# Spreading the forget-gate sums of eight attention heads to all partitions: products and copies, or DMAs from one row

## What is computed

```python
def forgetting_attention(q, k, v, f_logit):
    """logit[t,s] = q_t.k_s / sqrt(Dh) + sum_{s<j<=t} log sigmoid(f_logit_j), for s <= t."""
    logf = jax.nn.log_sigmoid(f_logit.astype(jnp.float32))
    c = jnp.cumsum(logf, axis=1).transpose(0, 2, 1)
    ...
        logits = jnp.einsum('bqhd,bkhd->bhqk', qb, kb).astype(jnp.float32) * scale
        logits = logits + c[:, :, q0:q1, None] - c[:, :, None, :q1]
        logits = jnp.where(causal[None, None], logits, -jnp.inf)
        p = jax.nn.softmax(logits, axis=-1).astype(v.dtype)
        outs.append(jnp.einsum('bhqk,bkhd->bqhd', p, vb))
```

## Time and profile before

| | us |
|---|---|
| median of 3 timed runs | 2202.22 |
| lowest and highest | 2200.33, 2208.86 |
| the profiled execution | 2198.62 |
| its span on the core | 2196.8 |
| TensorE busy in it | 2107.9 (96%) |
| VectorE busy | 1241.9 (57%) |
| ScalarE busy | 832.4 (38%) |
| POOL busy | 204.6 (9%) |

### The profile page before, as it was taken

The page is one execution under the profiler, slowest core; times in us unless marked ns, Lnnn a source line. Parts: engine busy times, 40 slices in busy tenths (PEclk is TensorE's granted clock), DMA queues, the critical chain, the costliest instruction groups (busy, mean ns, idle before and its releaser), DMA issues.

```text
span 2196.8 us, 26815 instructions
## 1 busy us (share of the span) xinstructions
PE 2107.9 (96%) x10738; PEld 1653.3 (75%) x10738; DVE 1241.9 (57%) x1891; ACT 832.4 (38%) x1335; POOL 204.6 (9%) x173
## 2 busy tenths in 40 slices
PE   6999999999999999998999999999999989999998
PEld 5777887678878876665788888777777767888886
DVE  4555665436677777887544344465675754443443
ACT  4344554345323233125423223344554543232231
POOL 2222001011000004452000000100000000000001
PEclk9999999999999999999999999999999999999999
DMA  5212322124677762652242332122121221422321
GB/s 175 77 58 96 117 96 77 39 77 154 240 251 251 269 244 89 151 148 74 77 135 93 99 96 96 52 78 58 43 74 49 62 92 58 134 96 96 96 96 39
DMA packets 217530, 241.74 MB, mean 110 GB/s; under 512 B 9920, under 2 KB 203968, under 8 KB 211264
## 3 DMA queue, kind: packets, MB, share of 16 engines
q1 hardware_dynamic: 207616, 229.58, 32.0%
q10 hardware_dynamic: 9792, 10.45, 1.9%
HBM read 229.01 MB, written 2.10 MB: 105 GB/s over the span
## 4 chain that ended last, share of the span: by engine, by line
PE 82%; DVE 8%; ACT 6%; issue 2%; ACTq 1%; DMA 1%; POOL 1%; DVEq 0%; SPq 0%; POOLq 0%
PE bank L1170 22%; PE bank L1171 22%; PE bank L1172 22%; PE bank L1191 2%; PE bank L1193 2%; PE bank L1192 2%; DVE wL L1751 1%; PE bank L1368 1%; PE bank L1345 1%; PE bank L1241 1%; DVE hX L2093 1%; PE bank L1254 1%; PE bank L1234 1%; PE bank L1296 1%; ACTq L1595 1%
## 5 line engine op out<-in xcount | busy, mean ns | idle before, releaser
L1170 PE MATMUL bank<-hH,wH 128*128 128x512 f32 (+1 forms) x1672 | 663.8, 397 | 33.1 <-DVE hL L1757 16.2
L1171 PE MATMUL bank<-hL,wH 128*128 128x512 f32 (+1 forms) x1672 | 647.7, 387 | 0.0
L1172 PE MATMUL bank<-hH,wL 128*128 128x512 f32 (+1 forms) x1672 | 647.7, 387 | 0.0
L1404 ACT ACTIVATE wH<-raw 128x1024 fp32r<-128x1024 f32 (+1 forms) x378 | 335.0, 938 | 363.4 <-PE bank L1172 267.6
L1751 DVE TENSOR_TENSOR wL<-raw,wH 128x1024 fp32r<-128x1024 f32 (+1 forms) x342 | 377.7, 1147 | 165.7 <-ACT wH L1404 165.6
L1170 PEld LDWEIGHTS bank<-hH,wH 128*128 128x128 f32 x1672 | 316.2, 189 | 124.4 <-issue 51.3
L1172 PEld LDWEIGHTS bank<-hH,wL 128*128 128x128 f32 x1672 | 315.9, 189 | 64.9
L1171 PEld LDWEIGHTS bank<-hL,wH 128*128 128x128 f32 x1672 | 316.4, 189 | 62.9 <-issue 2.4
L1170 PE MATMUL bank<-hidH,wH 128*128 128x512 f32 x768 | 299.2, 390 | 3.4 <-DVE hidL L1911 3.4
L1172 PE MATMUL bank<-hidH,wL 128*128 128x512 f32 x768 | 298.8, 389 | 0.0
L1171 PE MATMUL bank<-hidL,wH 128*128 128x512 f32 x768 | 298.8, 389 | 0.0
(11 more groups left out here) (214 smaller groups left out, 2059.3 us busy)
## 6 DMA issues: line engine op xcount, KB each, us to landing
raw<-in_mlp SPq DMA_DIRECT2D x64, 1024.0 KB, 5.3
araw<-in_ada_w SPq DMA_DIRECT2D x48, 1024.0 KB, 5.0
raw<-in_w_ff SPq DMA_DIRECT2D x32, 1024.0 KB, 7.3
raw<-in_hgrn_in SPq DMA_DIRECT2D x32, 512.0 KB, 3.8
raw<-in_w_in SPq DMA_DIRECT2D x12, 1024.0 KB, 5.3
raw<-in_conv_in SPq DMA_DIRECT2D x16, 512.0 KB, 4.8
u<-uc ACTq DMA_DIRECT2D x120, 67.5 KB, 3.1
raw<-in_w_mv SPq DMA_DIRECT2D x4, 1024.0 KB, 5.7
```

The costliest lines, as they stand in the source:

```text
L1170: mm(out, wH[:, s, m:m + 128], xh[:, k, 0:width], start=k == 0, stop=False)
L1171: mm(out, wH[:, s, m:m + 128], xl[:, k, 0:width], start=False, stop=False)
L1172: i = mm(out, wL[:, s, m:m + 128], xh[:, k, 0:width], start=False, stop=k == KB - 1)
L1404: do(wH[:, s, c], raw[:, r, c], ACT.Copy).then_inc(*s_whi.up(n, x))
```

## The change

The eight products and the eight copies go, with `sel` and its load. Item `decay` is now a DMA on SP's queue: it reads the row of head h from `tmp` (a source of one partition, repeated 128 times by a step of 0) and writes it to 128 partitions. There are four places for a head: the two slots of `cneg` and the last two key blocks of `qk` (12 + sc, that is 14 and 15), which are not filled until the key columns of the last heads are computed; `ev_k` for those two blocks now waits for POOL's last bias of heads 6 and 7. The DMAs of pair p + 1 are appended when pair p starts, those of pair 0 just before. The third and fourth pair's wait until POOL is done with the head that had the place. The first two `rel` loads move one pair forward. The minus sign, which `sel` gave, is moved into `ev_gate`: same instructions with other operations.

The diff, without the parts that only rename:

```diff
+    def decays(self, p):
+
+        for h in (2 * p, 2 * p + 1):
+            self.chead[0, h] = 2 * (p % 2) + h % 2
+            self.do("decay", h=h, sc=self.chead[0, h], n=p // 2 + 1,
+                    cfree=(("pool", "bias", (0, h - 4, 3)),) if p > 1 else ())
+
+    def rels(self, p):
+        for h in (2 * p, 2 * p + 1):
+            self.chead[1, h] = h % 2
+            self.do("rel", h=h, sc=h % 2, after=(("dve", "max", (1, h - 2, 3)) if p else ("pool", "bias", (0, h + 4, 3)),))
+
     def pairs(self):
+        self.decays(0)
         for g in range(2):
             for p in range(4):
-                for h in (2 * p, 2 * p + 1):
-                    sc, free = self.cslots.get()
-                    self.chead[g, h] = sc
-                    if g == 0:
-                        b, bfree = self.lin.get()
-                        self.do("decay", h=h, sc=sc, cfree=free, b=b, after=bfree)
-                        self.lin.put(b, ("act", "decay", h))
-                        if h == 7:
-                            self.tmps.put(self.gate_slots[0], ("mm", "decay", 7))
-                    else:
-                        self.rel_n[h] = 1 + sum(self.chead[1, x] == sc for x in self.rel_n)
-                        self.do("rel", h=h, sc=sc, after=free)
-                        self.do("rel_mask", h=h, sc=sc)
+                if g == 0 and p < 3:
+                    self.decays(p + 1)
+                    if p == 2:
+                        self.tmps.put(self.gate_slots[0], ("decay", 6), ("decay", 7))
+                elif g == 0:
+                    self.rels(0)
+                else:
+                    if p:
+                        self.rels(p)
+                    for h in (2 * p, 2 * p + 1):
+                        self.do("rel_mask", h=h, sc=h % 2)
                 for i in range(4):
                     yield self.pair(g, p, i)
...
+        def gates(sc):
+            return cneg[:, sc, :] if sc < 2 else qk[:, 12 + sc, :]
...
-                elif kind == "decay":
-                    h = it["h"]
-                    pe.wait_ge(*s_dve.at("gate", 6))
-                    pe.wait_ge(s_sel, LANDED)
-                    mm(banks[it["b"]][:], view(sel, h, [[0, 128]]), tmp[0:8, plan.gate_slots[0], :], start=True,
-                       stop=True).then_inc(*s_mm.up("decay", h))
...
-                elif kind == "decay":
-                    h = it["h"]
-                    act.wait_ge(*s_mm.at("decay", h))
-                    for ev in it["cfree"]:
-                        act.wait_ge(*event(ev))
-                    do(cneg[:, it["sc"], :], banks[it["b"]][:], ACT.Copy).then_inc(*s_act.up("decay", h))
...
+                    if it["blk"] > 5:
+                        dve.wait_ge(*s_pool.at("bias", (0, it["blk"], 3)))
...
-                    e.tensor_scalar(z, z, vec[0:8, VEC["bf"]:VEC["bf"] + 1], None, ADD).then_inc(*s_dve.up("gate", 2))
+                    e.tensor_scalar(z, z, vec[0:8, VEC["bf"]:VEC["bf"] + 1], -1.0, ADD, MUL).then_inc(*s_dve.up("gate", 2))
...
-                    pool.wait_ge(*s_act.at("decay", u["h"]))
+                    pool.wait_ge(*decayed(u["h"]))
...
-            dma(sel[:], a["sel"]).then_inc(s_sel, LANDED)
...
+                elif kind == "decay":
+                    sp.wait_ge(*s_dve.at("gate", 6))
+                    for ev in it["cfree"]:
+                        sp.wait_ge(*event(ev))
+                    h = it["h"]
+                    dma(gates(it["sc"]), view(tmp, T * plan.gate_slots[0], [[0, 128], [1, T]], p0=h, parts=1)).then_inc(
+                        s_decay[it["sc"]], LANDED)
```

More of the change, by code:

```diff
@@ L370, in pair @@
             self.do("bias", u=u)
-            if g == 0 and i == 3:
-                self.cslots.put(u["sc"], ("pool", "bias", u["id"]))
         yield
@@ L376, in pair @@
         for u in us:
-            if g == 1 and i == 3:
-                self.cslots.put(u["sc"], ("dve", "max", u["id"]))
             self.lin.put(u["b"], ("dve", "max", u["id"]))
@@ L1007, in build_program @@
         s_rel = [sem(f"s_rel_landed{i}") for i in range(2)]
-        s_vec, s_cst, s_msk, s_strip, s_sel = (sem(f"s_{n}_landed") for n in ("vec", "cst", "msk", "strip", "sel"))
+        s_decay = [sem(f"s_decay_landed{i}") for i in range(4)]
+        s_vec, s_cst, s_msk, s_strip = (sem(f"s_{n}_landed") for n in ("vec", "cst", "msk", "strip"))
         s_mem = [sem(f"s_mem_landed{i}") for i in range(4)]
@@ L1050, in build_program @@
             mstrip = sb(st, "mstrip", [128, 512])
-            sel = sb(st, "sel", [8, 8])
             macc = sb(st, "macc", [128, 256])
@@ L1127, in event, with decayed @@
                 return s_x[ev[1]], LANDED
+            if ev[0] == "decay":
+                return decayed(ev[1])
             return flags[ev[0]].at(*ev[1:])
+        def decayed(h):
+            return s_decay[h % 4], LANDED * (h // 4 + 1)
+        def gates(sc):
+            return cneg[:, sc, :] if sc < 2 else qk[:, 12 + sc, :]
         def levels(h, lev):
@@ L1150, in tensor_program @@
                 for ev in it.get("after", ()) if kind in ("scores", "turn", "mscores", "mturn", "mvalues", "close",
-                                                          "close_rows", "busy", "decay", "mem_close", "ada_sum",
+                                                          "close_rows", "busy", "mem_close", "ada_sum",
                                                           "conv_pe", "ln_mean", "ln_rest", "diag", "level",
@@ L1777, in vector_program @@
                     dve.wait_ge(s_vec, LANDED)
-                    e.tensor_scalar(z, z, vec[0:8, VEC["bf"]:VEC["bf"] + 1], None, ADD).then_inc(*s_dve.up("gate", 2))
+                    e.tensor_scalar(z, z, vec[0:8, VEC["bf"]:VEC["bf"] + 1], -1.0, ADD, MUL).then_inc(*s_dve.up("gate", 2))
                     dve.wait_ge(*s_act.at("gate", 3))
-                    e.scalar_tensor_tensor(out=g, in0=z, scalar=0.0, in1=g, op0=MIN, op1=SUB).then_inc(*s_dve.up("gate", 5))
+                    e.scalar_tensor_tensor(out=g, in0=z, scalar=0.0, in1=g, op0=MAX, op1=ADD).then_inc(*s_dve.up("gate", 5))
                     dve.wait_ge(*s_dve.at("gate", 5))
@@ L2156, in pool_program @@
                         pool.wait_ge(*event(ev))
-                    pool.wait_ge(*s_act.at("decay", u["h"]))
+                    pool.wait_ge(*decayed(u["h"]))
                     pool.wait_ge(s_strip, LANDED)
-                    e.tensor_tensor(L, cneg[:, u["sc"], 0:w], mstrip[:, 384 - 128 * i:512], ADD).then_inc(
+                    e.tensor_tensor(L, gates(u["sc"])[:, 0:w], mstrip[:, 384 - 128 * i:512], ADD).then_inc(
                         *s_pool.up("bias", u["id"]))
                 elif kind == "rel_mask":
-                    pool.wait_ge(s_rel[it["sc"]], LANDED * plan.rel_n[it["h"]])
+                    pool.wait_ge(s_rel[it["sc"]], LANDED * (it["h"] // 2 + 1))
                     e.memset(cneg[0:64, it["sc"], 448:512], NEG).then_inc(*s_pool.up("rel", it["h"]))
@@ L2346 @@
         "mstrip": strip,
-        "sel": -np.eye(8, dtype=f32),
         "dw4": dw4.reshape(128, 4 * QUADS * KB),
```

6 lines of the change are left out of this document (3 added, 3 removed).

## The result

The changed kernel took 2204.9 us, the median of 12 runs (2200.48 to 2209.72), the kernel before 2200.7 us in 12 runs beside them (2197.48 to 2208.86). The ratio is 1.0021, 95% interval 1.0011 to 1.0030: 4.6 us slower, between 2.4 and 6.6 (the two medians differ by 4.2). The forecast was 2207 us and +5.8 us. The change is smaller than the 0.5% that the prediction called tellable, but the interval lies above 1, so the kernel did become slower. The profiled execution took 2204.49 us with a span of 2202.7 us, against 2198.62 and 2196.8 before: +5.9 us.

The account below looks back on a forecast made before the run. TensorE was taken as the bound, with 82% of the chain of waits. A delay of 8.1 us plus 1.5 for the clock less 3.8 for products gave +5.8 on 2201.3, so 2207 us, range 2193 to 2216.

Parts of the forecast that it names:

- What is removed: On TensorE, four groups of two gate-sum products before the head pairs, 1.91 us each: 7.6 us off the path.
- The time of a one-row DMA: On SP's queue, each 256 KB read of one tmp row takes 9.8 us; ends considered were 2.6 and 11.3 us.
- the trend of u<-uc: SBUF copy from 32 partitions, 236 GB/s at full share against 370 from 128: fewer source rows slower, pointing to 9.8 us.
- The chain of landings: Piece 7 lands at 62.6 us, heads behind it, piece 8 at 105.4; TensorE's value products then start 8.1 us later.
- The clock: After TensorE idles some 10 us before the value products, its clock drops to the lower level, costing 1.5 us.
- The sum: Whole kernel: 8.1 us delay plus 1.5 clock less 3.8 for the two product groups still to come, +5.8 us.
- SP is free again before 68.85 us: the issue itself delays no fetch.: On SP's queue, four row DMAs issue 0.34 us apart from about 57.7 us, so piece 8's fetch is issued undelayed.
- Afterwards the transfers keep up: Behind piece 8, heads 4 to 7 and pieces 9 to 12 land in time; holding the last key evictions costs nothing.
- The fast row: Rival: one row is read fast, under 6.8 us per transfer, all covered; -7.6 us, 2193.7 us; chance 0.17.
- The slower one: Rival: engines contend for one row, from 11.1 us per transfer; +11.8 us at 11.3, +18.6 at 13; chance 0.15.
- SP's order: Rival: SP stalls at head 4 or 6 until POOL's biases, weight fetches behind; under 1 us; chance 0.03 with anything else.
- The break-even: Row DMAs ahead of piece 8: at 8.3 us per transfer the wait gives back what the removed products save.

Follow-up runs that it names:

- e1_wide: Changed kernel with each of the eight DMAs reading the slot's 128 rows instead of one row 128 times: 2191.8 us, ratio 0.9952 to the kernel before.
- e7_near: Changed kernel with each head's DMA cut into four, reading neighbouring rows 0, 1, 2, 3: 2204.2 us, ratio 1.0013 to the kernel before.
- e8_far: Changed kernel with each head's DMA cut into four, reading rows 0, 4, 8, 12: 2192.4 us, ratio 0.9957 to the kernel before.
- e6_busy: Changed kernel with eight unused products on TensorE just before the value products it waits for: 2200.1 us, ratio 1.0000 to the kernel before.
- e3_actq: Changed kernel with the eight row DMAs issued on ScalarE's queue, weight pieces staying on SP's: 2206.2 us, ratio 1.0014 to the kernel before.
- e10_before: The kernel before, unchanged, run and profiled a second time: 2201.1 us, ratio 0.9991 to the kernel before.
- e2_late: Changed kernel with the DMAs of heads 2 and 3 moved behind the fetch of weight piece 8: 2192.2 us, ratio 0.9954 to the kernel before.
- e12_late_again: Repeat of the changed kernel with heads 2 and 3 behind weight piece 8: 2194.3 us, ratio 0.9966 to the kernel before.
- e9_spaced: Changed kernel with row DMAs spread, at most two between two weight pieces, heads 0 and 1 before piece 6: 2196.2 us, ratio 0.9971 to kernel before.
- e11_rows: Kernel before with its eight products over all 128 rows of tmp, selector zero beyond row 7: 2197.5 us, ratio 0.9983 to the kernel before.
- e5_five: Changed kernel with a fifth one-row DMA, to a place nobody reads, ahead of weight piece 8: 2213.2 us, ratio 1.0057 to the kernel before.
- e4_half: Changed kernel with heads 0 to 3 by products and copies again, heads 4 to 7 by DMAs: 2197.8 us, ratio 0.9991 to the kernel before.

## Why the prediction was right, step by step

**What is removed.** Four groups, 7.6 us: right. The cleanest reading is e1_wide, where the same place stands 7.8 us earlier.

**The time of a one-row DMA.** 9.8 us was taken, from one of 16 engines' share of 427 GB/s; it took 9.2 us in the mean (9.6, 9.6, 8.4), at 26 to 30 GB/s. The choice between the ends, by the trend of u<-uc, was the step that decided the sign, and it held, in part by luck: a copy from 32 partitions says nothing sure of one row. The reason given with it, one engine's rate, is not what e7_near and e8_far show: the limit goes by groups of source partitions. Both give a sixteenth of the total, so the number could not tell them apart. The estimate of 9.6 us by the Trainium skill's page "SBUF — State Buffer" (section "Door 1: The DMA port swizzle") was the nearer one, and the two pairs of rows that were 9.6 apart hit it.

**The chain of landings.** Piece 7 at 62.6: measured 62.6. Head 0 at 72.4: 70.2, since part of it moved beside piece 7. Head 1 at 82.2: 79.8, so the maximum of the second head came at 80.37 and the transposes at 85.1 and 85.75, with 0.37 us of waiting and 0.44 more behind them, and not near 88. Head 3 at 101.8: 97.8. Piece 8 at 105.4: 102.1, 4.3 us behind head 3 (3.6 predicted). TensorE's value products 8.1 us late: 5.05. **This is the term that was mis-sized**, by 3.1 us: 2.2 for the overlap of head 0 with piece 7, which the sum had one after the other, 1.8 for the three later rows (27.6 us in place of 29.4), less 0.7 for piece 8 and 0.2 from ScalarE's copy to the products.

**The clock.** 1.5 us predicted from one wait in the trace before: 2.2 by the shift of the value products, and 2.2 by e6_busy. The wait taken was not the only one with a fall behind it: the trace before has the one at 32.7 us too, with a clock of 0.65 from 34 to 38 us. Here the clock stood at 0.50 from 100 us to 108 and at 0.62 to 110, so longer at the low level than behind 890 us, where the idle time was a small part of this.

**The sum.** Predicted 8.1 + 1.5 - 3.8 = +5.8. By the rows of after 5.05 + 2.2 - 3.9 = +3.4 at 157 us. The profiled execution adds 1.6 by the clock at the memory attention's wait and 0.9 elsewhere. The ratio's +4.6 us lies between. So the mechanism was as forecast, but that 2207 came so near is in part luck: the largest term was 3 us too high, and the sum left out 1 to 2 us further on.

**"SP is free again before 68.85 us: the issue itself delays no fetch."** The premise failed. The fourth issue took 9.48 us, piece 8's 15.59 and piece 9's 10.46, against 0.34 to 0.37. Piece 8 went out 0.27 us later than before and piece 9 2.43 us later (84.80 for 82.37), and nothing waited for piece 9. So the conclusion held here, by luck: SP had nothing else to do, and with a free queue piece 8 landed only 2.3 us sooner (e3_actq). On ScalarE the same hold stops an engine that computes (15.38 us of idle time), though there it was hidden behind head 1.

**Afterwards the transfers keep up**: right. Heads 4 and 5 landed at 112.3 and 119.6 us (issued at 95.31 and 99.38), POOL took them at 127.09 without a wait for a DMA; no piece behind the eighth was waited for, and the evictions of the last key blocks were not held.

**The rivals.** The fast row is out by its landings. The slower one (11.1 us or more) is out too. SP's order cost nothing. The break-even was put at 8.3 us per row and not measured; e8_far, at about 85 GB/s, 3 us a head, shows the side on which all is covered.

## What to carry to other kernels

To spread one partition's row over all the others by DMA went at 26 to 30 GB/s here: 9.2 us in the mean for 256 KB. Count each such DMA as if it closed the DMA system for that time, also for loads on other queues, and put no more than two of them ahead of a fetch that is waited for; the same eight DMAs cost 4.6 us in one order and gained about 7 in another. If the source may lie on several partitions, rows 0, 4, 8 and 12 gave three times the rate of rows 0 to 3; no other distance was tried. And before positions in two profiles are compared, look for a place ahead of the edit where they differ already.

## What the runs showed of the hardware that I had not expected

- **An issue can hold its engine.** With rows under way, SP stood in one DMA issue for 9.48, 15.59 and 10.46 us, ScalarE for 6.77 and 9.60. In the kernel after the first three rows went out in 0.59 to 0.66 us each; on ScalarE only the first two were as quick. That some store of pending descriptors is full would fit; no run measured one.
- **A second queue does not let a load pass rows that were issued before it.** In e3_actq piece 8 was issued on an otherwise empty queue at 68.74 us, ahead of head 3 (72.84), and landed 31.1 us later, 2.5 us behind head 2 and 5.5 ahead of head 3.
- **A DMA share of 0.9 at 27 GB/s.** The busy share of the DMA engines says nothing of the bytes moved; that it counts waiting for the source would fit.
- **The clock behind a short wait is not settled by its length.** All 14 profiles have the wait ahead of the memory attention's value products. The clock stood at 1.00 behind waits of 1.53, 1.75, 1.79, 2.17 and 2.32 us (e10_before, e2_late, before, e8_far, e1_wide), and fell behind 1.99, 2.04, 2.05, 2.13, 2.49, 2.64, 2.65, 2.82 and 2.88 us (e3_actq, e12_late_again, after, e6_busy, e9_spaced, e7_near, e11_rows, e5_five, e4_half). The ranges overlap from 1.99 to 2.32, and each is one execution. The falls are alike, 0.57 to 0.61 over the four microseconds that begin 0.6 us into those products, and each costs 1.5 to 1.6 us: the next value products that wait come 20.0 us later without it and 21.5 to 21.6 with it.
- **The clock fell to 0.76 with TensorE busy throughout** (e4_half, 0.76 and 0.77 behind its two groups), which the three other profiles with such products do not repeat. The cause is open.
